# Two-block network on one core: 17 mixing panels per layer as split products, modulation steps moved out of the mixing

## What is computed

```python
h = rmsnorm(x, norm_mix)
(a_x, a_b, a_c, d_q, d_k, d_v, i_q, i_k, i_w, g_q, g_f, g_i, g_g, m_q, gate_logits) = split_cols(h @ w_in)
y_a = a_b * causal_conv3(a_c * a_x, conv_w)          # branch 0
# branch 1 (y_b): an index score from i_q, i_k, i_w picks 64 keys per row; softmax attention of d_q over them
# branch 2 (y_c): gated linear attention in chunks of 64 from g_q, g_f, g_i, gated by g_g ("hgrn")
# branch 3 (y_m): attention of m_q over a memory, whose keys and values are mem_n @ mem_w_kv
merged = sum(sigmoid(gate_logits)[n] * (branch[n] @ w_lift[n]) for n in range(4))
x = x + merged @ w_out
gate, up = split(rmsnorm(x, norm_ffn) @ ffn_w_up); x = x + (silu(gate) * up) @ ffn_w_down
```

## Time and profile before

| | |
|---|---|
| median of 3 runs | 2469.78 us |
| profiled execution: time, span | 2467.38 us, 2465.6 us |
| busy | PE 93%, DVE 51%, ACT 27%, POOL 2% |
| first mixing, second mixing | about 25 to 491 us, 704 to 1166 us |
| FFN 0, FFN 1, FFN 2, FFN 3 (from VectorE's first product to TensorE's last) | 509 to 696, 1183 to 1373, 1819 to 2001, 2273 to 2452 us |

### The profile page before, as it was taken

How to read it: one execution, slowest core, us unless ns; L and a number is a source line. 1 busy time by engine, 2 the same in 40 slices (tenths; PEclk the granted TensorE clock), 3 DMA queues, 4 the chain that set the end, 5 groups by cost and what they waited for, 6 DMA issues and landing times.

```text
span 2465.6 us, 33483 instructions
## 1 busy us (share of the span) xinstructions
PE 2293.0 (93%) x14158; PEld 1902.1 (77%) x14158; DVE 1259.1 (51%) x2224; ACT 659.3 (27%) x882; POOL 57.5 (2%) x79
## 2 busy tenths in 40 slices
PE   6999989999989999799999998898899989989997
PEld 5858768699978587686999687877489967546996
DVE  3341346688733413444888366546355553634544
ACT  1113320043301133200444153321143411003442
POOL 0000000001000000000000000000010000000000
PEclk9999989999999999899999998999899999999999
DMA  6433326678644332267785321110265542203551
GB/s 212 150 111 115 116 81 226 209 252 279 211 135 149 120 119 103 86 222 249 244 281 201 92 73 65 36 36 2 63 188 187 171 141 79 97 0 115 186 186 68
DMA packets 207754, 348.68 MB, mean 141 GB/s; under 512 B 20643, under 2 KB 111562, under 8 KB 207221
## 3 DMA queue, kind: packets, MB, share of 16 engines
q1 hardware_dynamic: 192704, 291.15, 34.9%
q0 software_dynamic: 14624, 55.31, 6.8%
q10 hardware_dynamic: 276, 0.08, 0.0%
HBM read 345.48 MB, written 1.05 MB: 141 GB/s over the span
## 4 chain that ended last, share of the span: by engine, by line
PE 75%; DVE 17%; ACT 5%; issue 2%; DMA 1%; SPq 0%; DVEq 0%; ACTq 0%
PE psum L375 53%; PE psum L716 20%; DVE ring_low L1042 4%; DVE A L1506 3%; DVE G L1169 2%; ACT high_weights L1035 1%; DVE wide_room L1169 1%; ACT A L819 1%; PE psum L434 1%; DVE A L1169 1%; DVE tmp L1169 1%; DMA ring<-in_w_in_dram 1%; PE psum L420 1%; PE psum L694 0%; DVE xn L1469 0%
## 5 line engine op out<-in xcount | busy, mean ns | idle before, releaser
L375 PE MATMUL psum<-hT,ring 128*128 128x256 f32 (+1 forms) x3472 | 689.4, 360 | 16.3 <-DVE G L1169 7.1
L375 PEld LDWEIGHTS psum<-hT,ring 128*128 128x128 f32 x3472 | 602.5, 196 | 92.7 <-DVE G L1169 7.3
L1042 DVE TENSOR_TENSOR ring_low<-ring,high_weights 128x2048 fp32r<-128x2048 f32 x124 | 284.2, 2292 | 169.6 <-ACT high_weights L1035 167.6
L716 PE MATMUL psum<-high_rows,high_weights 128*128 128x256 f32 x1280 | 364.1, 284 | 4.8 <-DVE ring_low L1042 4.8
L716 PE MATMUL psum<-high_rows,ring_low 128*128 128x256 f32 x1280 | 362.4, 283 | 0.0
L716 PEld LDWEIGHTS psum<-high_rows,high_weights 128*128 128x128 f32 x1280 | 242.5, 189 | 7.0 <-issue 6.3
L716 PEld LDWEIGHTS psum<-high_rows,ring_low 128*128 128x128 f32 x1280 | 244.7, 191 | 0.0
L1035 ACT ACTIVATE high_weights<-ring 128x2048 fp32r<-128x2048 f32 x124 | 237.8, 1917 | 3.9
L1506 DVE SCALAR_TENSOR_TENSOR A<-A,silu_c 128x256 f32<-128x256 f32 x392 | 190.1, 485 | 14.0
L716 PE MATMUL psum<-yT_low,high_weights 128*128 128x256 f32 x640 | 181.2, 283 | 0.0
L716 PE MATMUL psum<-x2T_low,high_weights 128*128 128x256 f32 x640 | 180.1, 281 | 0.0
(11 more groups left out here) (409 smaller groups left out, 2485.5 us busy)
## 6 DMA issues: line engine op xcount, KB each, us to landing
ring<-in_w_in_dram SPq DMA_DIRECT2D x36, 2048.0 KB, 7.7
ring<-in_ffn_w_dram SPq DMA_DIRECT2D x66, 1024.0 KB, 5.3
A<-in_mod_w_dram POOLq DMA_DIRECT2D x48, 1024.0 KB, 7.7
ring<-in_ffn_w_up_dram SPq DMA_DIRECT2D x44, 1024.0 KB, 5.3
ring<-in_ffn_w_down_dram SPq DMA_DIRECT2D x22, 1024.0 KB, 6.9
ring<-in_w_lift_dram SPq DMA_DIRECT2D x16, 1024.0 KB, 8.4
ring<-in_ab_w_in_dram SPq DMA_DIRECT2D x7, 2048.0 KB, 7.9
ring<-in_hy_w_in_dram SPq DMA_DIRECT2D x6, 2048.0 KB, 8.0
```

The source lines that it names most:

```text
L375: return pe.eng.matmul(out, lhsT, rhs, start=(k == 0), stop=(k == n - 1))
L716: ins = pe.eng.matmul(out, lhs[a], rhs[b], start=first and n == 0, stop=last and n == 2)
L1042: v.eng.tensor_tensor(low, whole, high.bitcast(F32), ALU.subtract).then_inc(*v.mark(f"w_lo/{l}.{i}"))
```

## The change

Nine projection panels (a_c, a_b, i_q, d_q, g_f, g_q, g_i, g_g, m_q) and the eight gate panels of each layer are multiplied as split products; a_x, small, m_k, m_v, the lifts and out stay fp32. A panel is cut into four parts (of 128x1024), 68 per layer, numbered in the order of `SPLIT_PANELS` (a_c 0 to 3, ..., m_q 32 to 35, gate n.half from 36 + 8n + 4half). Each part's high lies in one of a few rooms (five, then three from part 40, then six from part 51). ScalarE makes highs in `prepared(l, form, h)`, VectorE lows in `lows(l, form, h)`; both are calls written by hand at points of their programs, and each goes on up to the first part that `parts_open` holds back. The rows hT are split once per layer (rows_hi, rows_lo). small is moved ahead of a_c. The order of memory rooms changes with it (merged rows now lie in hT, y of branches 0 and 2 share a room, memory rows in work).

The modulation steps leave the mixing. FFN 0 has steps 0 to 11 (one in each j, two in j = 9; steps 0 to 7 have two rows), FFN 1 steps 12 to 27 (two in j = 0 to 4), FFN 2 steps 28 to 47 (two in j = 0 to 8). The scan is done in two halves with a constant of half the width (256 KB less to load).

```diff
-        plan += [f"{n}{l}" for n in ("a_x", "a_c", "a_b", "small", "i_q", "d_q", "g_f", "g_q", "g_i", "g_g", "m_q")]
+        plan += [f"{n}{l}" for n in ("a_x", "small", "a_c", "a_b", "i_q", "d_q", "g_f", "g_q", "g_i", "g_g", "m_q")]
...
-    two = 16 - FFN_STEPS
-    return [24 * l + 8 + i for i in ([2 * j, 2 * j + 1] if j < two else [two + j])]
+    first, twice = MODULATIONS[l]
+    at = lambda j_: first + j_ + sum(1 for z in twice if z < j_)
+    return list(range(at(j), at(j + 1)))
+MODULATIONS = {0: (0, (9,)), 1: (12, (0, 1, 2, 3, 4)), 2: (28, tuple(range(9)))}
...
+    for i in range(PARTS_IN_ALL):
+        if i < first_part["gate{}.0.1"]:
+            rooms_ = ("a", "b", 10, 4, 5)
+        elif i < FIRST_LATE:
+            rooms_ = ("a", "b", 10)
+        else:
+            rooms_ = ("a", "b", 10, 2, 8, 9)
...
+    def parts_open(l, form, h):
+        end = first_part[form] + h if form else 0
+        place_of = top["plan"].index
+        at = place_of(form.format(l) if form else f"a_x{l}")
+        for i in range(PARTS_IN_ALL):
+            late = i >= FIRST_LATE and (not form or first_part[form] < first_part["gate{}.1.1"])
+            if late or part_user[i][0] >= end or any(place_of(z) >= at for z in top["loaded_after"][split_part(l, i)[0]]):
+                return i
+        return PARTS_IN_ALL
...
+        def split_ready(l, i):
+            pe.wait_ge(*reached(f"mix_lo/{l}.{i}"))
...
+        def product(out, lhs, rhs, first, last):
+            for n, (a, b) in enumerate(((0, 0), (0, 1), (1, 0))):
+                ins = pe.eng.matmul(out, lhs[a], rhs[b], start=first and n == 0, stop=last and n == 2)
+            return ins
+        def split_unit(form, l, u, label):
+            b = take(label)
+            for c in range(2):
+                i = first_part[form] + 2 * u + c
+                wh, wl, used = split_ready(l, i)
...
+                for k in range(KD):
+                    ins = product(b[:, c * SEQ:(c + 1) * SEQ], (wh[:, k, :], wl[:, k, :]), (rows_high[:, k, :], rows_low[:, k, :]),
+                                  k == 0, k == KD - 1)
...
+        def split_tokens(name, l):
+            labels = [f"{name}_ready/{l}.{t}" for t in range(MT)]
+            b = [take(label) for label in labels]
...
@@ merge_unit
-            for c in range(2):
-                for k in range(KD):
-                    ins = mm(b[:, c * SEQ:(c + 1) * SEQ], w[:, k, (2 * u + c) * P:(2 * u + c + 1) * P],
-                             hT[:, k, :], k, KD)
-            ins.then_inc(*pe.mark(label, [used] if u else []))
+            split_unit(f"gate{{}}.{n}.{half}", l, u, f"gate_ready/{l}.{n}.{q}")
@@ tensor: mixing
-                    if (n, q) != (2, 0):
-                        modulation_summed(pe, banks, 24 * l + 4 * (n - 2) + q - 1)
...
-            modulation_summed(pe, banks, 24 * l + 7)
@@ act_program
+            prepared(l, f"gate{{}}.{n}.{q // 2}", 2 * (q % 2) + 1)
...
+        def split_high(l, i):
+            a.wait_ge(*reached("panel " + name))
+            if before_ >= 0:
+                a.wait_ge(*reached(f"half/{l}.{before_}"))
...
+            copy(high, whole, f"mix_hi/{l}.{i}")
@@ dve_program
+        def lows(l, form, h):
+            while lows_done[l] < parts_open(l, form, h):
+                i = lows_done[l]
+                name, whole, high, low = split_part(l, i)
+                v.wait_ge(*reached(f"mix_hi/{l}.{i}"))
+                tt(low, whole, high.bitcast(F32), ALU.subtract, f"mix_lo/{l}.{i}")
+                lows_done[l] += 1
...
         def merge(l, n, q):
+            lows(l, f"gate{{}}.{n}.{q // 2}", 2 * (q % 2) + 1)
...
+                    if i in (1, 5):
+                        lows(l, ("g_f{}", "g_i{}")[t], 1 + 2 * (i // 5))
...
-                    i = 24 * l + 4 * (n - 2) + q
-                    if (n, q) != (2, 0):
-                        modulation_done(v, i - 1)
-                    modulation_scaled(v, i)
...
+        if l == 2:
+            top["gains"](range(3, 5))
@@ gpsimd
+                if n:
+                    pool.wait_ge(*reached("sumsq/ffn2.1"))
+                    for i in range(first_modulation(2), first_modulation(3)):
+                        modulation_in(i)
```

More of the change, by code:

```diff
@@ L368, in first_block, with split_part @@
     S = lambda l, n: PA[:, n + l:n + l + 1]
+    SPLIT_PANELS = ["a_c{}", "a_b{}", "i_q{}", "d_q{}", "g_f{}", "g_q{}", "g_i{}", "g_g{}", "m_q{}"]
+    SPLIT_PANELS += [f"gate{{}}.{n}.{half}" for n in range(4) for half in range(2)]
+    BY_TOKEN = ("g_i{}", "g_g{}")
+    PARTS_IN_ALL = 4 * len(SPLIT_PANELS)
+    first_part = {name: 4 * i for i, name in enumerate(SPLIT_PANELS)}
+    FIRST_LATE = first_part["gate{}.1.1"] + 3
+    part_room, part_user, last_user = [], [], {}
+    for i in range(PARTS_IN_ALL):
[5 more added lines that the diff above has]
+            rooms_ = ("a", "b", 10, 2, 8, 9)
+        r = min(rooms_, key=lambda z: (last_user.get(z, -1), rooms_.index(z)))
+        part_room.append(mix_high[:, "ab".index(r), :] if r in ("a", "b") else work_high[:, r, :])
+        part_user.append((last_user.get(r, -1), r))
+        last_user[r] = i
+    def parts_open(l, form, h):
[7 more added lines that the diff above has]
+        return PARTS_IN_ALL
+    def split_part(l, i):
+        form, h = SPLIT_PANELS[i // 4], i % 4
+        name = form.format(l)
+        if form in BY_TOKEN:
+            ks, cols, k = slice(2 * h, 2 * h + 2), slice(0, HALF), 2
+        else:
+            ks, cols, k = slice(0, KD), slice(h * P, (h + 1) * P), KD
+        whole, low = (panel_view(z, top["slot"][name])[:, ks, cols] for z in (ring, top["ring_low"]))
+        return name, whole, part_room[i].rearrange("p (k c) -> p k c", k=k), low
     def tensor(pe, banks):
@@ L508, in tensor @@
             ins.then_inc(*pe.mark(f"small_ready/{l}.1", [used]))
-            transposed("i_q", l, None)
+            for name in ("a_c", "a_b"):
+                split_transposed(name, l)
+            if l == 0:
+                for t in range(MT):
+                    norm_turned("mem", t)
+            split_transposed("i_q", l)
             def rotate(label, src, need):
@@ L546, in tensor @@
                     ins.then_inc(*pe.mark(f"q_sum_ready/{l}"))
[L547 to L550, removed]
+                    split_transposed("g_f", l)
+                    split_transposed("g_q", l)
+            split_tokens("g_i", l)
+            split_tokens("g_g", l)
             for t in range(MT):
@@ L1249, in dve_program @@
             v.wait_ge(*v.own())
+            label = f"small_ready/{l}.1"
+            e.tensor_copy(dvw[:, :, :], take(label)[:, 0:SEQ].rearrange("p (t c) -> p t c", t=2)[:, :, 0:72]).then_inc(*v.mark(f"dvw/{l}", ["read " + label]))
+            v.wait_ge(*v.own())
             for u in range(2):
+                lows(l, "a_c{}", 2 * u)
                 label = f"a_c_ready/{l}.{u}"
@@ L1267, in dve_program @@
                     norm_out("mem", t, PA[:, 32:40])
-            label = f"small_ready/{l}.1"
-            e.tensor_copy(dvw[:, :, :], take(label)[:, 0:SEQ].rearrange("p (t c) -> p t c", t=2)[:, :, 0:72]).then_inc(*v.mark(f"dvw/{l}", ["read " + label]))
-            v.wait_ge(*v.own())
+            lows(l, "i_q{}", 2)
             label = f"k_sum_ready/{l}"
@@ L1329, in dve_program @@
                 W = P * (t + 1)
+                if t == 0:
+                    lows(l, "g_g{}", 3)
                 b = take(f"logits_ready/{l}.{t}")
@@ L1384, in dve_program @@
             cum = A3[:, 1024:2048]
-            e.tensor_tensor_scan(cum, consts["chunk_scan"], A3[:, 0:1024], 0.0, ALU.mult, ALU.add).then_inc(*v.mark())
-            v.wait_ge(*v.own())
+            for half in range(2):
+                cc = slice(half * HALF, (half + 1) * HALF)
+                e.tensor_tensor_scan(cum[:, cc], consts["chunk_scan"], A3[:, cc], 0.0, ALU.mult, ALU.add).then_inc(*v.mark())
+                v.wait_ge(*v.own())
             c3 = cum.rearrange("p (c t) -> p c t", t=CHUNK)
@@ L1481, in ffn_dve @@
             if l == 1 and j == 0:
-                top["gains"](range(3))
+                top["gains"](range(2))
             if l == 1 and j == CTX_SCALED:
@@ L2500, in convolve @@
                     f"{label}/{n}" if c else None)
-        gains(range(3, 5))
+        gains([2])
         for t in range(MT):
```

170 lines of the change are left out of this document (130 added, 40 removed).

## The result

The changed kernel takes 2484.43 us (median of 8 runs, 2476.86 to 2485.05) against 2472.25 us before: a ratio of 1.0047, interval 1.0036 to 1.0058. It is slower by 0.5%: 12 us between the medians, 17.2 us between the two profiled spans (2482.8 against 2465.6). I had forecast 2467 us. The time is inside the range, the sign is wrong.

The account below looks back on a forecast made before the run. The chain that ended last was 75% TensorE, 17% VectorE. Terms +1.0 + 24.4 + 20.9 - 5.0 - 31.0 - 8.4 = +1.9 us gained from 2467.4 gave 2465.5, about 2467 us as forecast; range 2443 to 2486.

Parts of the forecast that it names:

- The split product: Mixing products: a gate's unit of 256 columns takes 5.77 us, 1.14 us saved; g_i and g_g save about 1.2 us.
- Layer 0 up to merge (0, 1): Layer 0's first half: cheaper units save 23.1 us, a longer wait costs 1.24 us, nothing is late; net +21.8 us.
- The +1.0 us for the smaller table: Kernel start: the table loaded first is 256 KB smaller, all ahead of the first panel, so 1.0 us is gained.
- Merge (0, 2): Both layers: `parts_open` holds part 40 until behind newton and root on VectorE, TensorE waits 13.4 us; net -13.1 us.
- Memory and hgrn: Memory's logits to hgrn and on to merge (1, 3): lows lengthen the chain, that merge gives 1.1 back; net -0.3 us.
- The last eight merges: End of each mixing: cheaper merges without modulation sums gain 15.3 us in layer 0 and 12.1 us in layer 1.
- FFN 0, FFN 2 and the hand-over: Added modulation steps make VectorE the chain: FFN 0 -5.0 us, FFN 2 -31.0 us, the stretch behind FFN 2 -8.4 us.
- (a): First half of each layer: parts come late at some 3 places, about 16 us in all, 2482 us; chance 0.20.
- (b): FFN 2: VectorE's excess is absorbed, only TensorE's 8 us is paid, 23 us better, 2444 us; chance 0.12.
- (c): `parts_open` misread: lows 40 to 43 are made while m_k and m_v run, 31 us better, 2436 us; chance 0.05.
- (e): The kernel stalls at an unseen place, or the clock stays low after a wait; above 2480 us; chance 0.07.
- Its twin of a slow clock behind merge (0, 2): Clock stays low for 18 us behind that merge's wait, 7 us more per layer, above 2480 us; shares chance 0.07.

Follow-up runs that it names:

- the first edit: Changed kernel with ScalarE's two copies of a_x in layer 0 put ahead of the sine, cosine and logistic set-up; 2469.55 us, ratio 0.9991 to the kernel before.

## Why the prediction was right in its parts and wrong in its sign

**The split product.** Right. The merges of the last stretch are 9.11 us apart (388.79 to 397.89 in the timeline above; 9.22 forecast), so a unit is 5.66 us; the products stand about 0.118 us apart. The 109 ns that the formula of the Trainium skill gives (TensorE: Matmul & The Clock Gate, Back-to-back issue gap) would have made it 5.24 us, an estimate; no run here shows it for this form. The 0.06 us that I added for a part's wait is not there.

**Layer 0 up to merge (0, 1): the step that failed.** "The move of small ahead of a_c covers the first parts" is true for the parts and was all that I asked. I followed the parts through the queues of VectorE and ScalarE for *their* lateness. I did not ask what else stood behind the new work in these queues. Four lows of the rows and four of parts were put ahead of the constants of layer 0, the profile before shows ScalarE waiting for VectorE's argument there already (12.60 us, up to 39.00), and the next thing on ScalarE is the copy that frees a bank. The price is 7.21 us and 2 us of slow clock: 9.96 us by the run that takes it away. In that run the row gains 24.5 us (218.5 us in place of 242.96), as layer 1 does (24.2). The 21.8 of the forecast and the cheaper unit (20 x 0.1 us) are 23.9 of this. The changed kernel lacks 14.8 us of it in layer 0, 9.96 up to g_i and 4.7 behind it, and so gains 9.7. The +1.0 us for the smaller table failed too: the first panel's load set the start in both kernels (25.01 and 25.12), so there was nothing to gain.

**The clock in layer 0.** The rest of that row, 4.7 us, was no step of mine. Whether the change costs it in every execution is not shown; I come back to it in the last section.

**Merge (0, 2).** Right, to 0.02 us: the guard, the order on VectorE, the wait of 13.42 us. The ramp behind it cost 1.9 us in layer 0 and 2.4 in layer 1 (7.75 and 8.28 us from the first product to the lift, against 388.79 to 394.62, 5.83, in the steady stretch), where I took 2. The size came out, though the row it was read from stands behind the wait of 3.17 us in hgrn too, and not only behind the 6.42. The run with early parts gave back 29.7 us for both layers.

**Memory and hgrn.** I had -0.3 us with a bound of -3. With the two merges and the ramp taken as measured it is about -3.5 in layer 0, outside the bound, and -2.2 in layer 1. The two lows in the chain were right: from the wait ahead of hgrn to the next one 11.03 us became 13.21. The five lows behind y_c were "mostly under merge (1, 2)" as I had said: the stretch that has them was 21.53 us long and is 21.11 now, with a wait of 3.71 us at its end in place of 1.83. What failed is the 1.1 us that merge (1, 3) was to give back. The stretch from there to the last eight merges grew from 14.12 to 15.67 us in layer 0 and from 15.53 to 15.74 in layer 1: the granted clock in it is 0.78 in both layers, where it was 1.00 and 0.89.

**The last eight merges.** Right: +16.1 and +13.1 us against +16.0 and +12.5.

**FFN 0, FFN 2 and the hand-over.** Right to 0.4 us each, -5.4 and -39.0. In the second two misses cancel, which is luck: from its first mark to TensorE's end FFN 2 grew from 182.8 to 214.7 us, 1 us more than forecast, and the hand-over lost 7.1 and not 8.4, since the slow clock behind it cost less than the 1.5 us that I took. The marks of FFN 2 are at 18.9 and 25.3 to 25.7 us as forecast from the earlier trace rows. The filter steps were told apart from the plain ones by two runs: without a modulation step they are 17.2 us, with one 21.4, with two 25.3 to 25.7, and only in the last case, where the step behind has two as well, is nothing made up there.

**The rivals.** (a) put late parts at three places of each layer. No part was late before merge (0, 2), so its mechanism is out, though its place (the first half) and its size (16 us) came near, which is luck. (b) and (c) are out by the same rows that bear the forecast. (e), a stall at a place that I didn't see, is what happened; it had 0.07. Its twin of a slow clock behind merge (0, 2) did not. The slow clock that cost 4.7 us came ahead of that merge, and 3.9 us more of the miss lie in FFN 1, the second block's first layer and the rest, where I had forecast nothing; they were not followed.

## What to carry to other kernels

When helper work is put into the queue of an engine, walk down that queue to the next instruction that frees something (a bank, a room, a semaphore that another engine stands at), also where the new work itself is early enough. One-time set-up in the first layer is such a queue, and the second layer won't show it. Periodic work that is to be hidden goes where the idle time of its engine is larger than one step of it, and one step per place: 12 steps in FFN 2 cost 5.6 us in its window, 20 cost 33.

## What the runs showed of the hardware

The same instructions over the same data can differ by 5 us in one place through the clock alone. The changed kernel and the one with eight steps in layer 1's mixing have identical code up to FFN 0, and both enter the stretch from the attention's products to the memory's sums behind the same wait of 1.95 us. The windows (columns as above):

```profile
232.18:258.38 26.20, 26.20 (x92) 17.29 (x92) 2.39 (x5) 2.75 (x4) 0.00 (x0) 0.81 0.34 118
```

```profile
231.12:252.51 21.39, 21.39 (x92) 13.39 (x92) 2.39 (x5) 2.74 (x4) 0.00 (x0) 1.00 0.41 145
```

The same 92 records take 26.20 us at a granted clock of 0.81 (part of the time at 1.2 GHz) and 21.39 us at 1.00 (2.4 GHz throughout). TensorE was not idle within either. Why one execution was granted the full clock there and the other not was not settled; what the engine did before it, two waits of about 1 us and one of 1.95, is the same in both. The 4.7 us of the first edit are of this kind, but 4.1 of them lie in two stretches. The first, ahead of the one in the windows (208.52 to 229.58 in the changed kernel, behind the wait of 0.85 us) takes 18.50 us in the kernel before and 18.51 with a_x's copies first, both at a granted clock of 1.00, and 21.06 at 0.85 in the changed kernel. The second, that of the windows, takes 24.57 and 24.70 us at 0.86 in those two, and 26.20 at 0.81 in the changed kernel. A long wait in layer 0 doesn't bring this by itself: the run with small behind a_b has one of 8.37 us and then 18.50 and 24.69. The profiles of the runs with parts 40 to 42 early and with split products only have 26.0 and 26.2 us in the second stretch, as the changed kernel. So it is partly a matter of the single execution, and of the same order as the 8 us by which the changed kernel's runs spread (2476.86 to 2485.05). A term of a few us behind a cluster of short waits therefore belongs into the range, not into the sum.
